# Forget heads' values: from token tiles ahead of the attention to feature tiles between its steps

## The reference

```python
D_MODEL, SEQ, HEAD_DIM = 1024, 512, 64
N_HEADS_DIFF, N_HEADS_FOX = 4, 8          # "diff" heads (two maps, values 128 wide), forget heads (values 64 wide)

def forgetting_attention(q, k, v, log_f):          # per block of 128 queries
    c = jnp.cumsum(log_f, axis=1)
    logits = q @ k.T * HEAD_DIM ** -0.5 + (c_q - c_k)      # causal
    return softmax(logits) @ v                             # v: (tokens, 64) of each head

def first_block(x, ...):                            # DEPTH = 2 layers
    for l in range(DEPTH):
        h = rms_norm(x, attn_pre_g[l])
        qa, ka, va, qb, kb, vb, f_logit = jnp.split(h @ w_in[l], split_at, axis=-1)   # 6 x 512 columns, then 8
        qa, ka = partial_rotary(qa), partial_rotary(ka)
        oa = rms_norm(diff_attention(qa, ka, va, lam), diff_sub_g[l]) * (1.0 - lam_init)
        log_f = log_sigmoid(f_logit + forget_bias[l])
        ob = forgetting_attention(qb, kb, vb, log_f)
        x = x + rms_norm(concatenate([oa, ob]) @ w_out[l], attn_post_g[l])
        h = rms_norm(x, ffn_pre_g[l])
        x = x + rms_norm((silu(h @ w_gate[l]) * (h @ w_up[l])) @ w_down[l], ffn_post_g[l])
    return x
```

## Time and profile before

| | us |
|---|---|
| median of 3 runs | 2260.12 (2259.81 to 2261.11) |
| the profiled execution, its own time | 2263.99 |
| its span (first to last instruction) | 2262.7 |
| layer 0: from the rotary products' end to the first scores | 50.0 to 111.5 |
| layer 0: first scores to the first tile of `out` | 111.5 to 273.2 |
| layer 1: first scores to the first tile of `out` | 771.5 to 933.4 |
| TensorE busy, share of the span | 94% |
| granted TensorE clock, mean | 0.979 |

### The profile page before, as it was taken

How to read it: one execution, slowest core, us unless ns; L and a number is a source line. 1 busy time by engine, 2 the same in 40 slices (tenths; PEclk the granted TensorE clock), 3 DMA queues, 4 the chain that set the end, 5 groups by cost and what they waited for, 6 DMA issues and landing times. The chain is left out here.

```text
span 2262.7 us, 25574 instructions
## 1 busy us (share of the span) xinstructions
PE 2133.4 (94%) x10364; PEld 1712.6 (76%) x10364; DVE 988.6 (44%) x1833; ACT 815.3 (36%) x1574; POOL 226.7 (10%) x256
## 2 busy tenths in 40 slices
PE   6899899999998999999999999988898999999997
PEld 5667688888887767688888877767665788888886
DVE  6265453323336364453323346645355444333333
ACT  4145443223224355342222334342355434222222
POOL 3003410000000004210000000000254201000000
PEclk9899999999999999999999999989899999999999
DMA  6521123233332312123333222313411232323321
GB/s 154 109 75 57 57 80 106 89 98 103 93 98 71 94 47 75 62 84 97 98 98 93 98 80 75 93 29 84 103 48 38 61 117 84 102 89 101 100 89 69
DMA packets 273721, 192.10 MB, mean 85 GB/s; under 512 B 22060, under 2 KB 241364, under 8 KB 273604
## 3 DMA queue, kind: packets, MB, share of 16 engines
q1 hardware_dynamic: 268704, 177.76, 27.3%
q0 software_dynamic: 4752, 12.67, 2.5%
q10 hardware_dynamic: 148, 0.04, 0.0%
HBM read 186.21 MB, written 4.23 MB: 84 GB/s over the span
## 5 line engine op out<-in xcount | busy, mean ns | idle before, releaser
L584 PE MATMUL bank<-h_features,weights_hi_lo 128*128 128x512 f32 (+1 forms) x5160 | 1138.2, 381 | 17.1 <-DVE weights_hi_lo L917 7.9
L584 PEld LDWEIGHTS bank<-h_features,weights_hi_lo 128*128 128x128 f32 x5160 | 933.7, 190 | 206.7 <-issue 14.6
L917 DVE TENSOR_TENSOR weights_hi_lo<-weights,weights_hi_lo 128x1024 fp32r<-128x1024 f32 (+1 forms) x337 | 402.7, 1199 | 703.7 <-ACT weights_hi_lo L1521 703.1
L1521 ACT ACTIVATE weights_hi_lo<-weights 128x1024 fp32r<-128x1024 f32 (+1 forms) x337 | 340.9, 1016 | 401.2 <-PE bank L626 352.4
L624 PE MATMUL bank<-weights_hi_lo,hidden 128*128 128x512 f32 x528 | 205.4, 389 | 0.0
L625 PE MATMUL bank<-weights_hi_lo,hidden 128*128 128x512 f32 x528 | 205.4, 389 | 0.0
L626 PE MATMUL bank<-weights_hi_lo,hidden 128*128 128x512 f32 x528 | 205.4, 389 | 0.0
L1637 ACT ACTIVATE hidden<-arena 128x512 fp32r<-128x512 f32 x66 | 41.7, 632 | 300.0 <-DVE arena L1068 300.0
L1930 POOL TENSOR_SCALAR arena<-arena,row_stats 128x256 f32<-128x256 f32 (+5 forms) x140 | 126.3, 913 | 198.7 <-DVE row_stats L992 70.9
L1902 POOL TENSOR_TENSOR h_features<-arena,h_features 128x512 fp32r<-128x512 f32 x24 | 30.7, 1278 | 992.0 <-ACT h_features L1549 992.0
L1068 DVE TENSOR_TENSOR arena<-bank,arena 128x512 f32<-128x512 f32 x66 | 45.6, 692 | 181.3 <-PE bank L584 181.3
(11 more groups left out here) (335 smaller groups left out, 2063.8 us busy)
## 6 DMA issues: line engine op xcount, KB each, us to landing
weights<-in_w_in_dram SPq DMA_DIRECT2D x84, 512.0 KB, 3.9
weights<-in_w_gate_dram SPq DMA_DIRECT2D x66, 512.0 KB, 3.8
weights<-in_w_up_dram SPq DMA_DIRECT2D x66, 512.0 KB, 3.8
weights<-in_w_down_dram SPq DMA_DIRECT2D x60, 512.0 KB, 3.6
weights<-in_w_out_dram SPq DMA_DIRECT2D x24, 512.0 KB, 3.7
bias_rows<-decay_scratch POOLq DMA_DIRECT2D x16, 256.0 KB, 4.0
weights<-in_w_cmp_dram SPq DMA_DIRECT2D x16, 256.0 KB, 5.4
weights<-in_w_down_dram SPq DMA_DIRECT2D x12, 256.0 KB, 2.6
```

Of the source, the lines that this page charges most:

```text
L584: last = e.matmul(out_ap, l, r, start=(j == 0), stop=(j == len(pairs) - 1))
L917: e.tensor_tensor(pair_view(i, 1), raw_view(i), pair_view(i, 0).bitcast(F32), ALU.subtract).then_inc(done, tick(("split", i)))
L1521: e.activation(pair_view(i, 0), raw_view(i), ACT.Copy).then_inc(done, tick(("hi", i)))
```

## The change

The eight forget heads' values `vb` are no longer made as token tiles ahead of the attention. Four feature tiles (128 of the 512 columns each, two heads) stand in `fill` at 18, 22, 26 and 30. VectorE copies each into one of the two rotary buffers (`diag_rstd`, `rotary_scratch`), one index later TensorE turns it in four 128x128 transposes, and ScalarE copies the turned tile into V. The first weighing of each pair of forget heads waits for that copy. `logs` moves ahead of `va`.

```diff
--- before.py
+++ after.py
@@ -89,7 +89,8 @@
 
 
 FILL = sorted([(4 * p - 4 + i, c, p) for p in range(1, 4) for i, c in enumerate((C_QA, C_KA))]
-              + [(4 * p - 3 + 2 * i, c, p - 4) for p in range(4, 8) for i, c in enumerate((C_QB, C_KB))])
+              + [(4 * p - 3 + 2 * i, c, p - 4) for p in range(4, 8) for i, c in enumerate((C_QB, C_KB))]
+              + [(4 * p + 2, C_VB, p - 4) for p in range(4, 8)])
 FILL_AT = {at: (c, m) for at, c, m in FILL}
 
 LAG = 6
@@ -345,7 +346,6 @@
             plan_features((s, "qk"), w, C_QA, P)
             plan_features((s, "qk"), w, C_KA, P)
             plan_tokens((s, "va"), w, [(C_VA, C_VA + 512)], ND)
-            plan_tokens((s, "vb"), w, [(C_VB, C_VB + 512)], ND)
             for _, c, m in FILL:
                 plan_features((s, "qk"), w, c + m * P, P)
             for half in range(2):
@@ -677,6 +677,8 @@
                         for j in range(len(u.turned)):
                             lane = dve if turned_by_vector(u, j) else act
                             pe.wait_ge(lane.done, lane[*u.name, "pt", j])
+                        if u.kind == "fox":
+                            pe.wait_ge(act.done, act[u.name[0], "values", u.p - N_DIFF])
                     for r, c0, c1, l, moving, start, stop in g.products:
                         last = e.matmul(out_ap[r, c0:c1], l, moving, start=start, stop=stop)
                     last.then_inc(done, tick(g.name))
@@ -730,13 +732,12 @@
                     feature_tile((s, "qk", C_KA), HT)
                     rotate(C_QA, 0)
                     rotate(C_KA, 0)
-                    token_tiles((s, "va"), 512, HT, ND)
                     out_ap = bank((s, "logs"))
                     pe.wait_ge(dve.done, dve[s, "log f"])
                     for t in range(NT):
                         last = e.transpose(out_ap[:, N_FOX * t:N_FOX * (t + 1)], NEGC[:, t * P:(t + 1) * P], CST[0:N_FOX, 0:N_FOX])
                     last.then_inc(done, tick((s, "logs")))
-                    token_tiles((s, "vb"), 512, HT, ND)
+                    token_tiles((s, "va"), 512, HT, ND)
                     out_ap = bank((s, "sums"))
                     pe.wait_ge(dve.done, dve[s, "logs"])
                     for t in range(NT):
@@ -747,6 +748,13 @@
                     def fill(at):
                         if at - 1 in FILL_AT and FILL_AT[at - 1][0] in (C_QA, C_KA):
                             rotate(*FILL_AT[at - 1])
+                        if at - 1 in FILL_AT and FILL_AT[at - 1][0] == C_VB:
+                            m = FILL_AT[at - 1][1]
+                            out_ap = bank((s, "values turned", m))
+                            pe.wait_ge(dve.done, dve[s, "value features", m])
+                            for t in range(NT):
+                                last = e.transpose(out_ap[:, t * P:(t + 1) * P], ROPE[m % 2][:, t * P:(t + 1) * P], IDENT)
+                            last.then_inc(done, tick((s, "values turned", m)))
                         if at in FILL_AT:
                             c, m = FILL_AT[at]
                             feature_tile((s, "qk", c + m * P), HT)
@@ -1172,15 +1180,12 @@
                     straight(C_KA, 0)
                     crossed(C_QA, 0)
                     crossed(C_KA, 0)
-                    for part, base in (("va", 0), ("vb", 512)):
-                        slabs_of((s, part), ND, 512, 1)
-                        for t in range(0, NT, 2):
-                            e.tensor_copy(V[:, t, base:base + 512], full((s, part, t))[:, :]).then_inc(done, tick())
-                            banks.leave(dve, (s, part, t))
-                        if part == "va":
-                            e.tensor_copy(FGT, full((s, "logs"))[:, 0:NT * N_FOX]).then_inc(done, tick((s, "logs")))
-                            banks.leave(dve, (s, "logs"))
-                    dve.also((s, "values"))
+                    e.tensor_copy(FGT, full((s, "logs"))[:, 0:NT * N_FOX]).then_inc(done, tick((s, "logs")))
+                    banks.leave(dve, (s, "logs"))
+                    slabs_of((s, "va"), ND, 512, 1)
+                    for t in range(0, NT, 2):
+                        e.tensor_copy(V[:, t, 0:512], full((s, "va", t))[:, :]).then_inc(done, tick((s, "values")))
+                        banks.leave(dve, (s, "va", t))
                     e.tensor_scalar(NEGC[:, :], full((s, "sums"))[0:N_FOX, :], -1.0, None, ALU.mult).then_inc(done, tick((s, "decay")))
                     banks.leave(dve, (s, "sums"))
                     dve.wait_ge(act.done, act[s, "values"])
@@ -1195,6 +1200,11 @@
                             splits_for((s, "qk", c + m * P))
                             if c in (C_QA, C_KA):
                                 straight(c, m)
+                            if c == C_VB:
+                                if m >= 2:
+                                    dve.wait_ge(pe.done, pe[s, "values turned", m - 2])
+                                e.tensor_copy(ROPE[m % 2], full((s, "qk", c + m * P))[:, :]).then_inc(done, tick((s, "value features", m)))
+                                banks.leave(dve, (s, "qk", c + m * P))
                         if at - 2 in HEAD_AT:
                             h = HEAD_AT[at - 2]
                             dve.wait_ge(act.done, act[s, "head rstd", h])
@@ -1677,21 +1687,25 @@
                     rope(C_QA, 0)
                     splits_for((s, "qk", C_KA))
                     rope(C_KA, 0)
-                    for part, base in (("va", 0), ("vb", 512)):
-                        slabs_of((s, part), ND, 512, 1)
-                        for t in range(1, NT, 2):
-                            e.activation(V[:, t, base:base + 512], full((s, part, t))[:, :], ACT.Copy).then_inc(done, tick((s, "values")))
-                            banks.leave(act, (s, part, t))
+                    slabs_of((s, "va"), ND, 512, 1)
+                    for t in range(1, NT, 2):
+                        e.activation(V[:, t, 0:512], full((s, "va", t))[:, :], ACT.Copy).then_inc(done, tick((s, "values")))
+                        banks.leave(act, (s, "va", t))
                     if layer == 0:
                         act.wait_ge(strips_written, 16)
 
                     def fill(at):
+                        if at - 1 in FILL_AT and FILL_AT[at - 1][0] == C_VB:
+                            m = FILL_AT[at - 1][1]
+                            e.activation(V[:, :, 512 + m * P:512 + (m + 1) * P], full((s, "values turned", m))[:, :].rearrange("p (t c) -> p t c", t=NT),
+                                         ACT.Copy).then_inc(done, tick((s, "values", m)))
+                            banks.leave(act, (s, "values turned", m))
                         if at in FILL_AT:
                             c, m = FILL_AT[at]
                             splits_for((s, "qk", c + m * P))
                             if c in (C_QA, C_KA):
                                 rope(c, m)
-                            else:
+                            elif c in (C_QB, C_KB):
                                 e.activation((QB if c == C_QB else KB)[:, m, :], full((s, "qk", c + m * P))[:, :], ACT.Copy,
                                              scale=SCALE if c == C_QB else 1.0).then_inc(done, tick((s, "qk", c, m)))
                                 banks.leave(act, (s, "qk", c + m * P))
```

## The result

| | kernel before | changed kernel |
|---|---|---|
| median, us | 2260.96 (2259.81 to 2263.02, 5 executions) | 2275.47 (2266.28 to 2275.88, 5 executions) |
| the profiled execution | 2263.99 | 2275.88 |
| ratio of the mean times | | 1.005, 95% interval 1.0034 to 1.0066 |

The changed kernel is slower, as forecast, but by 14.5 us by these medians and not by 7.1: 2275.5 lies above the range (2261.5 to 2271.5). Three of its five executions took 2275.5 to 2275.9, the other two 2269.05 and 2266.28. The second pair is where the forecast was (2267.2). So two things have to be explained: the parts that the change touches, and the 8 us between these two groups.

What follows compares the result with a forecast made beforehand. TensorE bounds the kernel (94% busy, attention steps nearly full), weight slabs layer 0's front. Layer 0 -19.9 + 2.2 + 23.4 = +5.7, layer 1 -22.0 + 23.4 = +1.4: +7.1 on 2260.12 gives 2267.2 us, range 2261.5 to 2271.5.

Steps and rivals of the forecast that it cites:

- Layer 0's front, -19.9 and +2.2: Ahead of layer 0's attention: scores start 19.9 us sooner, limited by weight slab 8; cold clock then costs 2.2 us.
- One for one: Layer 0's front: weight packets alternate singly with the 2 MB write's packets; some 240 of 512 through by 86 us.
- The first rival: Layer 0's front: slab 8 arrives at 85.7 as before, scores at 89.3; total +4.8 us, 2264.9; chance 22%.
- The tiles, 18.2 + 1.3: Each layer's attention: feature tiles at 18, 22, 26 cost 18.2 us; bank wait at index 19 and the rest 1.3.
- The fourth rival: Attention steps: PSUM ring waits at all four new tiles, 4.8 us per layer; total +14.1, 2274.2; chance 7%.
- the third: Attention steps: new tiles fill the 8.5 us of waits per layer; at best 5.7 us faster, 2254.4; chance 6%.
- The tile at 30, +3.9: End of each layer's attention: later maxima on VectorE delay GpSimd's scaling, 3.9 us for 6.1 of work.
- The clock at the end: Last weighing of each layer's attention: left at the low clock, 3.25 us instead of 1.73, as before.
- the second rival: End of attention: TensorE stays at 2.4 GHz, 2.0 us gained per layer; total +3.1, 2263.2; chance 20%, either front.
- Layer 1's front, -22.0: Ahead of layer 1's attention: the 96 `vb` matmuls, standing without a wait, leave TensorE's path, 22.0 us less.
- From first scores to `out`: Attention length after the change: 187 us in layer 0, 185 in layer 1 (161.9 + 23.4).
- The sum, +7.1: Whole kernel: layer 0 +5.7 and layer 1 +1.4, together +7.1 us; forecast 2267.2, chance 45%.

Runs made afterwards that it cites:

- e1: The changed kernel again, no edit: median 2271.09 us, ratio 1.0043, in two groups of five executions.
- e5: Kernel before with second-block attention banks freed sooner and the 2 MB `bias_scratch` write issued behind layer 0: 2243.37 us, ratio 0.9921.
- e6: Changed kernel with second-block attention banks freed sooner and the 2 MB `bias_scratch` write issued behind layer 0: 2252.98 us, ratio 0.9964.
- e8: Kernel before with second-block attention banks freed sooner and the 2 MB write issued within layer 0's attention: 2232.42 us, ratio 0.9873.
- e9: Changed kernel with second-block attention banks freed sooner and the 2 MB write issued within layer 0's attention: 2238.70 us, ratio 0.9894.
- e4: Changed kernel with gate and branch tiles of the second block's attention read out earlier, freeing PSUM banks: 2253.66 us, ratio 0.9967.
- e3: Kernel before with gate and branch tiles of the second block's attention read out earlier, freeing PSUM banks: 2248.29 us, ratio 0.9941.
- e10: Changed kernel with its PSUM bank ring turned by five, giving the second block's attention the kernel before's banks: 2267.64 us, ratio 1.0033.
- e2: Kernel before with 16 more matmuls (3.6 us) in a projection tile at the second block's start: 2266.57 us, ratio 1.002.
- e14: Kernel before with 24 more matmuls (5.4 us) in a projection tile at the second block's start: 2265.77 us, ratio 1.0019.

## Why the prediction was wrong

The direction was right and the steps on the changed parts held; one sentence under the total did not: "the difference is the same for both, so I add it to the median". It takes all that the change doesn't touch as running alike, and so puts it at nothing. The second block's attention, which has no changed line, ran 8.3 us longer in the profiled execution (44 us at the low clock where it was 27), and by the totals and the mean clock so it did in 8 of the changed kernel's 15 executions. The lower seven, 2265.6 to 2269.1, are where the forecast put all. Which group the median falls into was luck: by e1 alone it is 2271.09.

Point by point:
- *Layer 0's front, -19.9 and +2.2.* Scores at 92.64 (91.6), -18.85, or -19.3 against the layer's start; slab 8 at 89.07 (88, bounds 85.7 and 90); 2.2 us lost in the first steps, 1.8 of them in the first tile. One for one was right to the packet: of the 512 rows of slab 7 that share engines with the write 252 had come by 84 us, where the forecast had some 240 by 86. The first rival (slabs as before) is wrong. That the write is the cause is shown by e5, e6, e8 and e9. Of what "DMA: Bandwidth & Descriptors" of the Trainium skill says in "Queues, rings and completion order", the turns agree with this trace, the whole packet of some 9 to 17 descriptors at a turn does not: with as many rows of the weights as of the write in every 0.67 us, the turns are of one row.
- *The tiles, 18.2 + 1.3.* Measured 19.1 in either layer, the 1.16 us at index 19 among them. The fourth rival (the ring costs everywhere) is wrong, though its 2274.2 lies nearest to the measured median: at 22, 26 and 30 no wait is there that was not there before. So is the third (the tiles fill waits): the waits of 8.5 us were at other indices.
- *The tile at 30, +3.9.* +3.85 and +3.81 up to the last weighing, by the chain that was named: maxima 8.8 and scaling 10.3 us behind the scores (9.0 and 10.5 in the forecast).
- *The clock at the end.* I left it as before. In the first profile it stayed up in layer 0 (-1.5 at `out`), as in the second rival; in layer 1 the last weighing was at the low clock as before, 3.25 us, and the low stretch was shorter (933.5 to 940.3, before 925.2 to 935.5). Over the profiles it goes either way: from the scores of step 30 to `out` the changed kernel takes 20.4 or 21.9 us in most, the kernel before 18.1, 16.6 or 16.1, so the end costs from 2.3 (layer 0 here) over 5.4 (e9 against e8) to 5.8 (layer 1, e4 against e3), where the step's bounds were 1.9 and 5.4.
- *Layer 1's front, -22.0.* -21.74.
- *From first scores to `out`.* 185.4 us in layer 0 (187 forecast, less the 1.5 of the clock) and 184.7 in layer 1 (185). By its own signs of being wrong (a front that moves by other than 17 to 20, a layer 1 under 181 or over 189) the forecast of the layers stands.
- *The sum, +7.1.* +5.5 behind layer 1 in the first profile, +5.2 in e1, of which 0.5 and 0.3 stood before the layers began; +5.4 and +6.3 by the medians where the second block's attention was quiet (e4 against e3, e9 against e8). Between the layers and that stage some 2 us go again, 1.6 of them at the waits for the compression weights, which I had put at nothing too.
- *The range.* Its ends came from unknown prices in the changed parts alone. The rows for the rest were there: the stage stood at 0.92 with eleven waits of 0.87 to 1.55 us, each of which could bring a fall more or less; in the profile before they brought most of the 27 us at the low level, and 17 more cost 8. I read the clock at a layer's front and at its end and not in the stage with the most waits.

What stays open: why the kernel before, in 86 executions, never had the upper group. e1 and e10 show that it isn't the code of the stage or its banks, e3 and e4 that it needs its waits. That it is the moment at which the stage is entered isn't shown either. Counted from the program's start that moment decides nothing: the first scores stand at 1615.95 us in the profile with 44 us of low clock and at 1616.01 and 1615.88 in those of e1 and e10 with 27, and the kernel before, with work added, entered at 1615.52 (e2) and 1616.34 (e14) without it. Counted from the clock's own changes there is one difference in the rows: in e1 and e10 the clock fell 0.8 and 0.9 us ahead of the first scores, in the first profile 0.2 us behind them. But in e2 it fell 0.6 behind them and the stage had 27 us; it is one profile of the upper group, and no run varied this by itself.

## What to carry to other kernels

The stage here in which TensorE waited about 1 us every few tiles, at a mean clock near 0.9, was unstable: edits ahead of it moved the total by other than their own time, and an execution by chance as well. Where you see such rows, give the stage its own term in the range, compare stage by stage against the same instructions, and remove the waits (here a gain of 13 us) before judging effects under 0.5%. Beside a background DMA the rows count, not the bytes: a small-row weight load got as many packets here and an eighth of the bytes, so put such a write under a stage with few loads (here -16 us for the kernel before, e8 against e3). Work moved from ahead of an attention into its steps brought nothing here, where the steps were full; it only shared time with waits that stood right behind it.

## What the runs showed of the hardware

- The same program, on the same chip in the same session, took 2265.6 to 2267.9 or 2274.3 to 2276.4, nothing between (e1). Between one profile of either group the waits of the second block's attention are the same and its granted clock is not (0.92 and 0.88).
- Behind a wait of 0.95 and one of 0.58 us TensorE's next matmuls ran at the low level in one execution and at the high one in another, so the length of the wait alone doesn't decide.
- Waits cost more than their own time: in the profile of e3 the stage has 6.9 us less of waiting than before and is 15.5 us shorter, with 20.5 us less at the low clock.
- 71 packets of 4 KB and 72 of 512 bytes went through in 6 us, one and one in turn; the smaller ones don't catch up. A load of 512 KB in 512-byte rows landed 36.2 us after its issue beside the write (layer 0, changed kernel); in the kernel before the median over the 84 loads from that table of weights was 3.9.
